# Copying every second page of turned sample keys out of its PSUM bank on VectorE instead of ScalarE

## What is computed

```python
def diff_attend(q, k, v, q_pos, k_pos, lam):
    s = jnp.einsum('bqhcd,bkhcd->bhcqk', q, k) / math.sqrt(DIFF_HEAD_DIM)
    s = jnp.where(k_pos[None, :] <= q_pos[:, None], s, -jnp.inf)
    p = jax.nn.softmax(s, axis=-1)
    attn = p[:, :, 0] - lam * p[:, :, 1]
    return jnp.einsum('bhqk,bkhe->bqhe', attn, v)

def diff_sample(q, k, v, lam, k_pool, v_pool, page_table):
    k_past = k_pool[page_table].reshape(B, -1, DIFF_HEADS, 2, DIFF_HEAD_DIM)
    v_past = v_pool[page_table].reshape(B, -1, DIFF_HEADS, DIFF_V_DIM)
    ...
    return diff_attend(q, k_all, v_all, past + jnp.arange(T), jnp.arange(past + T), lam)
```

## Time and profile before

| what | value |
|---|---|
| median of three runs | 4987.94 us |
| profiled execution, its own time | 4989.02 us |
| its span in the trace | 4987.2 us |
| busy: TensorE / its weight loads | 83% / 72% |
| busy: VectorE / ScalarE / GpSimd | 41% / 35% / 10% |

### The profile page before, as it was taken

One profiled execution on the slowest core, in us unless ns is written; L12 is line 12 of the kernel. 1 busy time (PEld: TensorE's weight loads), 2 busy tenths in 40 slices (PEclk: granted clock), 3 DMA queues, 4 the chain that ended last, 5 costly groups with the idle time before them and its releaser, 6 DMA issues.

```text
span 4987.2 us, 113889 instructions
## 1 busy us (share of the span) xinstructions
PE 4126.7 (83%) x49138; PEld 3581.0 (72%) x49138; DVE 2025.7 (41%) x4512; ACT 1757.6 (35%) x3560; POOL 481.3 (10%) x264
## 2 busy tenths in 40 slices
PE   3999998878867888767989999968878688888495
PEld 2999997677764555546979999957777455555395
DVE  3111111666645545443231111146666445555234
ACT  3000001666655556541110000036666455556111
POOL 1222220000000000001032222200000000000200
PEclk9999998799998999877989999979999898989597
DMA  4211111111114444333222121111111333443333
GB/s 159 77 73 69 73 68 66 39 37 40 36 29 143 140 123 131 111 118 119 83 74 77 64 77 65 65 60 35 43 38 27 117 115 115 132 131 98 106 119 135
DMA packets 227647, 427.60 MB, mean 86 GB/s; under 512 B 32162, under 2 KB 137636, under 8 KB 212900
## 3 DMA queue, kind: packets, MB, share of 16 engines
q1 hardware_dynamic: 213316, 339.18, 21.6%
q10 hardware_dynamic: 13824, 81.07, 4.0%
HBM read 304.91 MB, written 123.80 MB: 86 GB/s over the span
## 4 chain that ended last, share of the span: by engine, by line
PE 69%; DVE 11%; ACT 8%; issue 4%; SPq 4%; DMA 3%; POOL 1%; ACTq 0%; DVEq 0%
PE psum L1801 10%; PE psum L1802 10%; PE psum L1803 10%; PE psum L1276 4%; PE psum L1300 4%; PE psum L699 3%; PE psum L1452 2%; PE psum L1454 2%; PE psum L1453 2%; PE psum L1290 2%; PE psum L1030 2%; ACT arena L1138 2%; PE psum L696 1%; PE psum L770 1%; PE psum L1043 1%
## 5 line engine op out<-in xcount | busy, mean ns | idle before, releaser
L1801 PE MATMUL psum<-x_hi,w_parts 128*128 128x416 f32 x2640 | 932.2, 353 | 59.2 <-POOL w_parts L1759 59.2
L1802 PE MATMUL psum<-x_lo,w_parts 128*128 128x416 f32 x2640 | 928.3, 352 | 0.0
L1803 PE MATMUL psum<-x_hi,w_parts 128*128 128x416 f32 x2640 | 927.4, 351 | 0.0
L1768 DVE TENSOR_TENSOR arena<-psum,arena 128x416 f32<-128x416 f32 x330 | 195.5, 592 | 1284.9 <-PE psum L1803 1284.7
L318 ACT ACTIVATE arena<-arena 128x256 f32<-128x256 f32 x16 | 8.2, 514 | 1543.5 <-DVE arena L442 1543.5
L1801 PEld LDWEIGHTS psum<-x_hi,w_parts 128*128 128x128 f32 x2640 | 497.2, 188 | 67.1 <-POOL w_parts L1759 62.5
L1803 PEld LDWEIGHTS psum<-x_hi,w_parts 128*128 128x128 f32 x2640 | 497.9, 189 | 6.6
L1802 PEld LDWEIGHTS psum<-x_lo,w_parts 128*128 128x128 f32 x2640 | 498.7, 189 | 4.4
L1206 DVE TENSOR_SCALAR_CACHE_REDUCE arena<-psum 128x512 f32<-128x512 f32 (+3 forms) x640 | 357.5, 607 | 322.2 <-PE psum L1276 211.8
L1300 PE MATMUL psum<-arena 128*128 128x128 f32 x2176 | 320.6, 290 | 43.2 <-ACT arena L1151 43.2
L1276 PE MATMUL psum<-arena 64*128 64x512 f32 (+3 forms) x1280 | 325.9, 614 | 19.5 <-DVE arena L1206 12.7
(11 more groups left out here) (337 smaller groups left out, 6723.4 us busy)
## 6 DMA issues: line engine op xcount, KB each, us to landing
out_proj_t<-arena ACTq DMA_DIRECT2D x66, 1040.5 KB, 4.2
arena<-in_cache_k SPq DMA_DIRECT2D x256, 256.0 KB, 2.7
arena<-in_cache_v SPq DMA_DIRECT2D x256, 256.0 KB, 3.0
arena<-in_w_in SPq DMA_DIRECT2D x66, 512.0 KB, 3.5
arena<-out_proj_t SPq DMA_DIRECT2D x32, 1024.0 KB, 7.2
arena<-out_proj_t SPq DMA_DIRECT2D x96, 257.0 KB, 3.1
m_raw<-mixed_t SPq DMA_DIRECT2D x10, 1664.0 KB, 7.2
x_res<-x_cur SPq DMA_DIRECT2D x10, 1664.0 KB, 18.2
```

Of the source, the lines that this page charges most:

```text
L1801: pe.matmul(bank[q % 8][:, 0:TG], w_hi[:, b % 3, k, :], x_hi[:, k, cols(g)], start=(k == 0), stop=False)
L1802: pe.matmul(bank[q % 8][:, 0:TG], w_hi[:, b % 3, k, :], x_lo[:, k, cols(g)], start=False, stop=False)
L1803: mm = pe.matmul(bank[q % 8][:, 0:TG], w_lo[:, b % 3, k, :], x_hi[:, k, cols(g)], start=False, stop=(k == KT - 1))
```

## The change

Pages with odd k are no longer copied out of bank 6 by ScalarE but by VectorE, with the same waits. TensorE's list, the loads and the bank stay as they are.

```diff
         def beside_scalar(act, b, k):
             if b is None:
                 return
-            if k < NP:
+            if k < NP and k % 2 == 0:
                 q = b * NP + k
                 act.wait_ge(k_turned, q + 1)
                 if q // 4 >= 2:
...
         def beside_vector(dve, b, k):
             if b is None:
                 return
+            if k < NP and k % 2:
+                q = b * NP + k
+                dve.wait_ge(k_turned, q + 1)
+                if q // 4 >= 2:
+                    dve.wait_ge(scored, q // 4 - 1)
+                dve.tensor_copy(kTs[:, q // 4 % 2, :, k % 4 * PG:(k % 4 + 1) * PG], TB.rearrange("p (h t) -> p h t", h=4)).then_inc(k_out, 1)
             if k == 2:
```

## The result

The changed kernel takes **5051.58 us** (median of 4 runs, 5042.36 to 5059.41) against 4987.4 us of the kernel before, run again beside it (4 runs, 4986.02 to 4997.24): a ratio of 1.0126 with an interval of 1.0111 to 1.014, 64 us slower. The forecast was 5076, with 5036 to 5112 as its range. The profiled execution took 5056.03 us, of which the span is 5054.2.

What follows compares the result with a forecast made beforehand. TensorE, busy 80% in the attention phases, was taken to set the pace. Terms summed to 10.9 us per head, 87 us over eight heads, on the profiled 4989.0; with the median 1.1 lower, 5076 us was named, range 5036 to 5112.

Steps and rivals of the forecast that it cites:

- Price of a copy: Time of one moved page copy on VectorE: 0.61 us, bounded below by 0.42 us.
- Pages 1, 3 and 5: First sequence, steps 1 and 2: TensorE gets later by +1.2 us for pages 1 and 3, +0.6 for page 5.
- Page 11: First sequence, step 4: copy behind the difference delays page 12's turn, two score blocks and the map; +4.2 us per head.
- Page 15: First sequence, step 5: copy ahead of tile 5's maximum delays the passes behind it; +0.4 us per head after slack.
- Page 3 of the second sequence: Step 10: copy behind the difference delays page 4's turn, two score blocks and the map; +2.25 us per head.
- the clock falls at more places: Rival: new pauses at steps 2, 10 and 12 lower TensorE's clock at two or three places per head; 5102 to 5115, chance 0.16.
- Page 9 of the second sequence: Step 12: copy behind the difference delays page 10's turn, with the whole delay staying; +2.45 us per head.
- Page 1 of the second sequence: No cost on VectorE; ScalarE's shorter queue ahead of the exponential of 1536 columns gives TensorE -0.2 us per head.
- Given back: Rival: lateness vanishes in TensorE's waits for cached values, half of the sum gone; 5032 us, chance 0.14.
- Faster by a shorter list on ScalarE: Rival: ScalarE's list shortens ahead of exponentials TensorE needs and direct waits halve; 13 us gained, 4976 us, chance 0.04.

Runs made afterwards that it cites:

- the filled kernel: The full change, plus 16 turns of the identity by TensorE while it waits for page 3's copy at step 10; 5045.29 us, ratio 1.012.

## Why the prediction was right, and where it was not

**The mechanism held.** The claim was that engines' busy shares say nothing here, that VectorE's list has two kinds of places, and that a copy behind the difference makes TensorE wait. One page alone (5013), the other ten (4981) and the same copies moved up (4992) show it. The sum was off by one at its end: 4989 and 87 less 1.1 is 5075, not 5076.

**Price of a copy.** Taken as 0.61 us, from the row that reads PSUM rather than the one that reads SBUF (0.42). Step 12 of the profile after shows it between its neighbours:

```profile
1818.36 0.55 DVE L1212 TENSOR_SCALAR_CACHE_REDUCE arena<-psum 128x384 f32<-128x384 f32 x1
...
1818.84 0.69 DVE L997 COPY arena<-psum 128x512 f32<-128x512 f32 x1
1819.45 0.14 DVE L1224 TENSOR_REDUCE arena<-arena 128x2 f32<-128x4 f32 x1
...
1820.45 1.69 DVE L1237 SCALAR_TENSOR_TENSOR arena<-arena 128x1408 f32<-128x1408 f32 x1
```

0.61 us to the next start, 688 ns in the mean of 128.

**Pages 1, 3 and 5.** Forecast 1.8 together, measured 1.3. Behind page 1 TensorE waited 0.63 us for the copy, as forecast, in six heads and not at all in the other two. Page 3 cost 0.47 in every head, and page 5 cost 0.6 in four heads and less in the others. Why these are less than a full copy there was not looked into.

**Page 11.** Forecast +4.2 within 2.85 to 4.65, measured +4.48. The slow end was right for the reason given: the eight scores behind the wait took 3.56 us, as in the earlier trace rows, and no longer beside VectorE's work.

**Page 15.** Forecast +0.4, not seen. The stretch is 45 us long and its clock varies by more than that: in the kernel before it took 43.3 us in one head, at a mean granted clock of 0.92, and 47.6 in another, at 0.82.

**Page 3 of the second sequence.** Forecast +2.25, measured +2.31, and then +1.60 more. This is the rival "the clock falls at more places", true at one place and not at the others. The argument against it was one idle time of 1.24 us that slowed nothing; the wait here was of 2.4 us, so that row could not speak for it. Other rows of the same head could have: behind page 15 TensorE stood 1.48 us at 1744.83 and 1.58 us at 1747.07, and the clock behind was 0.60. The same two waits were followed by 0.50 to 0.70 in all eight heads.

```profile
1747.00:1750.50 3.50, 3.28 (x13) 2.10 (x14) 2.55 (x10) 3.50 (x12) 0.00 (x0) 0.60 0.00 0
```

The term should have been in the sum.

**Page 9 of the second sequence: the step that failed.** The forecast put its copy behind the difference of 1408 columns, for +2.45. It is the wrong kind of place: step 12 has two score blocks, so at (12,1) j is below their number, and the copy stands ahead of the maxima and of the difference. The rows just above show it: scores 1818.36, copy 1818.84, difference 1820.45. The description of the list ahead of the prediction had both the rule and the two blocks; the step took them for one. It is an error of reading; nothing the chip did was needed for it. Measured, the stretch 9 to 10 changed by 0.00, and with this page among the ten moved alone nothing was lost (4981 us).

**Page 1 of the second sequence.** Forecast -0.2, measured -0.12 in every head.

So the total of 64 is close to 87 partly by luck: 20 us too much for page 9 and 13 us too little for the clock at step 10 cancel in part. Of the rest, the early pages were 4 us too dear and page 11 2 us too cheap, and the stretch behind page 15, forecast at +3 us, came out at -5.

**Given back.** The rival needed some 43 us of it, and no such amount is seen: TensorE's wait for values over the whole span is 73.8 us in the profile after and was 78.7 before, and with one page moved it was 79.0 (page 3) or 82.7 (page 11).

**Faster by a shorter list on ScalarE.** The Trainium skill ("TensorEngine Tiling (Array Packing)", section "PSUM Bottleneck") says to take results out of PSUM with both engines. Here that is worth between nothing and a quarter of a per cent, and only if each copy is put where VectorE is free: -0.13% with the ten free pages, -0.23% with six chosen ones, of which most is tied to no copy's place, and +1.26% by odd and even.

## What to carry to other kernels

Where each engine works through a list in order, the price of moving an operation is read from its new neighbours: what the engine waits for just ahead of it, and who waits for its result. Write down for each moved instruction which row stands before it, from the list itself, even when a rule seems to give it. And an idle time of the engine that sets the pace costs a second time when the clock behind it falls: look at the duration of the same instruction behind the wait, and if the wait can't be taken away, try to fill it.

## What the runs showed of the hardware beyond that

- A wait of 2.4 us in an otherwise busy stretch was followed in all eight heads by work at a lower granted clock: 0.51 to 0.69 in the profile after and 0.56 to 0.64 with page 3 moved alone, each in the mean of 3.5 us, between the levels of 1.2 and 2.4 GHz. The length of the wait does not decide it alone: the one of 1.24 us in the earlier trace rows changed nothing, one of 1.94 us was followed by a fall in five heads of eight, one of 1.48 and one of 1.58 close behind it by a fall in all eight, and in the kernel before one of 2.56 us, for values at 1841.60, by a clock of 1.00. The window of the profile after, at the place where the filled kernel shows 1.00:

```profile
1803.00:1806.50 3.50, 3.31 (x10) 1.90 (x12) 0.13 (x2) 1.93 (x6) 0.00 (x0) 0.52 0.14 22
```

- TensorE work whose result nobody reads holds the clock up: 16 turns of the identity, 1.91 us, put into the wait of 2.4 us kept the clock behind it at 1.00, and 12 of them at four places per head took 23 us off the kernel before.
- A copy 128 x 512 of fp32 out of PSUM takes 688 ns on VectorE and 596 on ScalarE; started back to back, 0.61 and 0.47 us apart.
- Single runs of one kernel lie up to 0.7% apart (the kernel before: 4973.59 to 5009.1 us in 23 runs), and in the kernels without filling the mean of the long stretch behind page 15 moved by up to 1.6 us per head. Effects under 0.2% could be tied to a place only where they stood in all eight heads.
